# Gather of four experts at a time in float32, scatter from one float32 y buffer, and a new layout of SBUF, in a two-layer decoder trunk with 64 routed experts

## The reference

```
y = concat(mixer heads, memory heads) @ w_out[i]
x = layer_norm(ALPHA * x + y)
aff = sigmoid(x @ w_router[i]); the best 8 of 64 experts within the best 4 of 8 groups
gates = aff of the chosen / their sum * 2.5
routed = sum over chosen experts of gate * ((silu(x @ w_gate[e]) * (x @ w_up[e])) @ w_down[e])
shared = (silu(x @ ws_gate) * (x @ ws_up)) @ ws_down
x = layer_norm(ALPHA * x + routed + shared)
```

## Time and profile before

| | |
|---|---|
| three runs | 1184.29, 1184.86, 1186.17 us |
| median | 1184.86 us |
| profiled execution, its span | 1183.3 us |
| PE busy | 1149.2 us (97%) |
| weight loads busy (PEld) | 688.0 us (58%) |
| VectorE, ScalarE, GpSimd busy | 347.2, 300.0, 56.4 us |
| read from HBM | 446.96 MB, 379 GB/s over the span |
| chain that ended last | PE 85%, DMA 9%, DVE 3%, ACT 1% |

### The profile page before, as it was taken

The page is one execution under the profiler, slowest core; times in us unless marked ns, Lnnn a source line. Parts: engine busy times, 40 slices in busy tenths (PEclk is TensorE's granted clock), DMA queues, the critical chain, the costliest instruction groups (busy, mean ns, idle before and its releaser), DMA issues.

```text
span 1183.3 us, 22174 instructions
## 1 busy us (share of the span) xinstructions
PE 1149.2 (97%) x8846; PEld 688.0 (58%) x8846; DVE 347.2 (29%) x912; ACT 300.0 (25%) x713; POOL 56.4 (5%) x100
## 2 busy tenths in 40 slices
PE   9999999999999999999999999999999899999995
PEld 6865755555555555554787647555555555555552
DVE  0445522222122212121523557221222222121224
ACT  1454222212122212121214533122221212221222
POOL 1431100000001000000011001000000010000000
PEclk9999999999999999999999999999999999999998
DMA  9945999999999999999990558999999999999995
GB/s 375 418 161 185 349 418 426 428 428 428 429 428 421 429 426 427 426 426 418 406 364 2 230 233 343 408 426 426 429 429 428 428 423 427 426 426 428 428 423 204
DMA packets 42732, 449.12 MB, mean 380 GB/s; under 512 B 4512, under 2 KB 4896, under 8 KB 14240
## 3 DMA queue, kind: packets, MB, share of 16 engines
q1 hardware_dynamic: 41648, 443.30, 89.8%
q10 hardware_dynamic: 1008, 4.73, 1.0%
HBM read 446.96 MB, written 1.05 MB: 379 GB/s over the span
## 4 chain that ended last, share of the span: by engine, by line
PE 85%; DMA 9%; DVE 3%; ACT 1%; issue 1%; DVEq 0%; SPq 0%; ACTq 0%
PE bank L1301 18%; PE bank L1328 17%; PE bank L1364 17%; PE bank L848 7%; PE bank L867 6%; PE bank L1372 5%; PE bank L906 4%; DMA store<-in_w_gate 4%; DMA store<-in_w_down 3%; DMA store<-in_w_in_b 2%; PE bank L1337 2%; PE bank L1196 1%; PE bank L1066 1%; PE bank L1077 1%; ACT work L1498 1%
## 5 line engine op out<-in xcount | busy, mean ns | idle before, releaser
L1301 PE MATMUL bank<-store,work 128*64 128x256 f32 x1984 | 227.8, 382 | 5.3 <-DMA store<-in_w_gate 5.3
L1328 PE MATMUL bank<-store,work 128*64 128x256 f32 x1952 | 225.3, 379 | 6.2 <-issue 6.2
L1364 PE MATMUL bank<-store,work 128*32 128x512 f32 x1888 | 218.4, 595 | 3.1 <-ACT work L1498 2.9
L1301 PEld LDWEIGHTS bank<-store,work 128*64 128x64 f32 x1984 | 137.0, 137 | 116.1 <-issue 41.1
L1328 PEld LDWEIGHTS bank<-store,work 128*64 128x64 f32 x1952 | 145.0, 137 | 75.7 <-issue 11.6
L2030 DVE SCALAR_TENSOR_TENSOR yhalf<-bank,gcol,yhalf 128x512 fp32r<-128x512 f32 x124 | 92.9, 751 | 219.1 <-ACT yhalf L1664 219.1
L2022 DVE TENSOR_TENSOR work<-work,bank 128x256 f32<-128x256 f32 x64 | 27.0, 422 | 346.9 <-PE bank L1328 346.9
L1664 ACT ACTIVATE yhalf<-bank,gcol 128x512 fp32r<-128x512 f32 x124 | 85.1, 688 | 172.1 <-PE bank L1364 172.1
L1364 PEld LDWEIGHTS bank<-store,work 128*32 128x32 f32 x1888 | 56.1, 109 | 122.4 <-issue 110.7
L1498 ACT ACTIVATE work<-bank 128x512 f32<-128x512 f32 (+4 forms) x177 | 78.0, 441 | 105.8 <-PE bank L848 47.3
L1498 ACT ACTIVATE back<-bank 128x128 fp32r<-128x128 bf16 x64 | 17.8, 278 | 282.0 <-PE bank L1269 282.0
(11 more groups left out here) (185 smaller groups left out, 822.7 us busy)
## 6 DMA issues: line engine op xcount, KB each, us to landing
store<-in_w_down SPq DMA_DIRECT2D x56, 2048.0 KB, 17.7
store<-in_w_gate SPq DMA_DIRECT2D x56, 2048.0 KB, 17.7
store<-in_w_up SPq DMA_DIRECT2D x52, 2048.0 KB, 19.2
store<-in_w_up SPq DMA_DIRECT2D x18, 1024.0 KB, 10.5
store<-in_w_gate SPq DMA_DIRECT2D x12, 1024.0 KB, 8.5
store<-in_w_in_b SPq DMA_DIRECT2D x3, 3072.0 KB, 22.4
store<-in_w_out SPq DMA_DIRECT2D x4, 2048.0 KB, 14.2
store<-in_w_down SPq DMA_DIRECT2D x6, 1024.0 KB, 11.7
```

The source lines that it names most:

```text
L1301: last = pe.matmul(gate_bank[slots_of(e), 0:HID], xg[:, k, slots_of(2 * j + e)], w[e][:, k, :], start=(k == 0), stop=(k == KT - 1))
L1328: last = pe.matmul(up_bank[slots_of(e), 0:HID], xg[:, k, slots_of(2 * j + e)], w[e][:, k, :], start=(k == 0), stop=(k == KT - 1))
L1364: last = pe.matmul(yb[half][rows_of(t, e), :], hT[b][:, f, slots_of(e, t)], w[e][:, f, half * 512:half * 512 + 512], start=(f == 0), stop= ...
```

## The change

x stays one float32 tensor in SBUF for the whole kernel; its columns stand in chunk order (the host permutes x, w_out, w_down, w_shared_down and the norm's rows, and the last norm writes the result back in column order into `x_out`). The float32r halves, `x_high`, `x_low` and GpSimd's sum are gone. The gather takes four experts at a time ("quad"), twice per octet, in units 1 and 3, each as float32 products with 128 moving columns; its four banks hold two chunks each. Slots lie by tile first in `xg`, so gate and up take one product per tile and expert: 32 stationary columns, 32 products each.

```diff
-                def gather(O, backs, bank_of_chunk=gather_bank):
+                def gather(Q, backs, banks_of=gather_bank):
...
-                        for t in range(TT):
...
-                            last = product(banks[bank_of_chunk[k]][:, t * 256:(t + 1) * 256],
-                                           [(xhalf[:, part, t, k * P:(k + 1) * P], hot8[:, t, :]) for part in range(2)])
+                        for i in range(2):
+                            k = 2 * c + i
+                            for t in range(TT):
+                                first = i * 256 + t * P
+                                last = pe.matmul(banks[banks_of[c]][:, first:first + P], x[:, t, k * P:(k + 1) * P], hot4[:, t, :],
+                                                 start=True, stop=True)
                         last.then_inc(s_("gathered"), 1)
...
                         for e in range(2):
-                            last = pe.matmul(gate_bank[slots_of(e), 0:HID], xg[:, k, slots_of(2 * j + e)], w[e][:, k, :],
-                                             start=(k == 0), stop=(k == KT - 1))
+                            for t in range(TT):
+                                last = pe.matmul(gate_bank[slots_of(e, t), 0:HID], xg[:, k, gathered_slots(j, e, t)], w[e][:, k, :],
+                                                 start=(k == 0), stop=(k == KT - 1))
```

```diff
-                    for n in range(2):
-                        for t in range(TT):
-                            pe.matmul(sums[2 * t + half][:], back[b][rows_of(t), :],
-                                      yhalf[rows_of(t), n, half * 512:half * 512 + 512], start=False, stop=False)
+                    for t in range(TT):
+                        pe.matmul(sums[2 * t + half][:], back[b][rows_of(t), :], y[rows_of(t), half * 512:half * 512 + 512],
+                                  start=False, stop=False)
...
                 def scatter(U, b):
-                    pe.wait_ge(s_("y_parted"), 2 * U + 2)
-                    for half in range(2):
-                        scatter_half(half, b)
+                    pe.wait_ge(s_("y_act"), U + 1)
+                    scatter_half(0, b)
+                    pe.wait_ge(s_("y_dve"), U + 1)
+                    scatter_half(1, b)
...
-                    ahead = j == OCT_PAIRS - 1
+                    ahead = b == 1
```

```diff
+            def keep_late(l, part, e):
+                w = (w_gate, w_up)[part][l, LATE_PAIR, :, e, :]
+                sp.dma_start(late_view(part, e), by_k(w)).then_inc(sem("late"), 16)
...
+                filled(sp, G[l, "y2"])
+                keep(l, 2, 0)
+                keep_late(l, 0, 0)
                 used(sp, (l, "out1"))
...
+                keep_late(l, 0, 1)
                 sp.wait_ge(sem("normed"), 2 * TT * l + TT)
-                load_up_apart(l)
                 keep(l, 1, 0)
...
+                sp.wait_ge(sem(f"shared_gu_{l}"), TT)
+                load_up_apart(l)
                 keep(l, 1, 1)
```

The last norm's second half writes with a stride:

```diff
+                    last = dve.scalar_tensor_tensor(out=by_column(x_out[:, t, :])[:, :, ms], in0=by_chunk(x[:, t, :])[:, :, ms],
+                                                    scalar=rstd[:, t, :], in1=by_chunk(lnrow[:, 1, :])[:, :, ms],
                                                     op0=ALU.mult, op1=ALU.add)
```

More of the change, by code:

```diff
@@ L183, in build_trunk @@
[L183 to L189 removed]
+        kT = work[:, 0:1536].rearrange("p (t n) -> p t n", n=SEQ)
@@ L618, in _ @@
                 if l == 0:
[L619 to L632 removed]
+                    first_layer()
+                else:
+                    second_layer(extra)
@@ L905, in out_part @@
                         done = y_done[n] = y_done[n] + 1
-                        last = pe.matmul(bank_at(g)[:], mixT[:, c, t * P:(t + 1) * P],
-                                         item_view((l, f"out{half}"), 512)[:, c, :], start=start, stop=(done == KT))
+                        last = pe.matmul(bank_at(g)[:], mixT[:, c, t * P:(t + 1) * P], wo[:, c, :], start=start, stop=(done == KT))
                         if done == KT:
@@ L1413, in unit @@
                     rs = 2 * O + j // 2
+                    late = shared == 0
+                    gathers = rs + 1
                     if shared in (1, 2):
                         pe.wait_ge(sem(f"shared_hT_{l}"), r * TT + (shared + 1))
-                    gate(U, O, j, rs, kept, place)
+                    gate(U, O, j, rs, kept, place, late)
                     if place == 0:
```

513 lines of the change are left out of this document (262 added, 251 removed).

## The result

The changed kernel takes 1258.49 us (median of 4 runs, 1258.12 to 1259.01), against 1184.76 us for the kernel before in the same rounds (1184.29 to 1186.17). The ratio is 1.0621, with a 95% interval of 1.0605 to 1.0636: 73.7 us more. The forecast was 1254 us, in a range of 1244 to 1280.

The account below looks back on a forecast made before the run. TensorE was taken as the bound nearly everywhere, DMA 10% slower in the loop but with a stock. Terms 47.0 + 42.8 - 9.3 - 11.5 - 0.9 + 1.5 = +69.6 us on 1184.9 gave 1254 us, range 1244 to 1280.

Parts of the forecast that it names:

- DMA's deficit: Expert loop: weight loads fall behind TensorE by 5.4 us per octet, 58.7 against 53.33 us; 0.4 after the change.
- Gather: Expert loops: 15 gathers per layer at 3.6 us replace 7 at 4.32; both layers +47.0 us.
- Scatter: Expert loops: float32 scatter takes 1.8 us instead of 1.12, in 62 units; +42.8 us.
- with the change of shape behind it 1.8: Scatter: four float32 pairs take 1.72 us, and 1.8 us with the change of shape that follows.
- Gate, up and down: Expert units: the change from 32 to 64 stationary columns goes, -0.15 us in each of 62 units; -9.3 us.
- Waits for weights: Expert loops: TensorE's waits before gate and up vanish as its octet grows to 58.3 us; -11.5 us.
- 3 MB less per layer are read inside the loop: Waits term: three kept matrices take 3 MB per layer out of the loop's loads, 7.3 us at 429 GB/s.
- The rest: Outside the main terms: -0.9 us of TensorE waits, +1.5 us for the last norm's strided write, no wait from load order.
- (a): Rival, gate and up: TensorE cannot take instructions fast enough, gate 3.90 us instead of 3.46; +56 us, 1310 us; chance 0.10.
- (b): Rival, expert loops: DMA is the true bound, 6.3 million bytes less save 14.7 us, 1170 us; chance 0.03.
- (c): Rival, gather and scatter: float32 forms cost about what float32r cost, 1170 us; chance 0.02.
- (d): Rival, gather or new load order: late copies or shared weights cause waits, +21 us, 1275 us; chance 0.10.

Follow-up runs that it names:

- the kernels with and without the shape: Kernel before with float32 scatter and wide float32 gather: with gate and up products of 32 columns 1251.49 us, without 1261.05 us.
- the two float32 experiments: Kernel before with one edit each: float32 scatter alone, 1219.70 us; float32 gather alone, still eight experts wide, 1211.06 us.
- the run without the kept matrices: Changed kernel without the three matrices it keeps for pair 24, which load as any other pair's: 1258.74 us.
- the experiment with 32 columns: Kernel before with gate and up products of 32 columns instead of 64, nothing else: 1192.72 us, ratio 1.0061.

## Why the prediction came out right, point by point

The verdict is the forecast's: TensorE sets the end, DMA's deficit vanishes, 1258.5 against 1254. By its terms:

- **Gather, +47.0.** 3.6 us was taken for a narrow one, 3.58 measured. Per layer 15 x 3.58 - 7 x 4.32 = +23.5 us. The first gather of layer 0, with gate's wait for the last copy, takes 133.82 - 129.14 = 4.68 us against 4.87; 4.6 was forecast. Together +46.6. The price was read from six records of another stage, and held.

```profile
129.14 3.81 PE L1311 MATMUL bank<-router_work,x 128*128 128x128 f32 x32
133.82 3.66 PE L1361 MATMUL bank<-ring,router_work 128*32 128x256 f32 x64 [0.87 <-DVE router_work L1792]
```

- **Scatter, +42.8.** This term was mis-sized. Measured are 1.92 us a scatter, not 1.8, so 0.80 and not 0.68 us a unit: 49.6 us, and 50.2 with the last half. Four pairs at 0.43 us were right in themselves. The step that failed is "with the change of shape behind it 1.8": 0.20 us lie beyond the four pairs, not 0.08, 7.4 us in 62 units. The prediction put the change of shape ahead of the scatter at nothing. The starts of the second and of the last pair, and of what follows, show both:

```profile
236.57 0.59 PE L1433 MATMUL bank<-router_work 64*128 64x512 f32 x2
...
237.43 0.60 PE L1433 MATMUL bank<-router_work 64*128 64x512 f32 x2
```

The pair in the middle takes 0.43 us (236.57 to 237.00, and to 237.43), the first one 236.57 - 236.04 = 0.53 and the last one 237.96 - 237.43 = 0.53: 0.10 us at each end. The float32r scatter of the kernel before has the same 0.10 at each end (medians of its 62: first pair 0.34 us, last 0.33, the others 0.23). So the 1.12 us held it already: four pairs at 0.23 are 0.93. The term's own upper bound (1.95 us, 51 us) held it.
- **Gate, up and down, -9.3.** Unit rows give -0.16, the kernels with and without the shape -0.154: 9.6 us. Right, and at the place named: down to gate lost 0.11 us, gate to up 0.06. The kernel before with this shape alone has the same steps, 3.46, 3.45 and 3.57 us. That it is the change between 32 and 64 columns that costs is argued from the place.
- **Waits for weights, -11.5.** All gone, as forecast, but there was more to give back: 13.9 us within the loops. The step took the list's lengths as the time lost; the two float32 experiments show that they are too short. (The first wait came at 305.65 us, 0.34 listed, and not at 315.) "3 MB less per layer are read inside the loop" is so, but the forecast did not need it: the stock holds without them, as the run without the kept matrices shows. An octet of 58.64 against 58.7 us was forecast as 58.3.
- **The rest, +0.6.** Together the stretches outside the loops changed by -0.3 us: before the first loop -0.3, between the loops -1.1, tail +1.1. The tail's strided operations are there as priced (2.06 us, and 2.10 for the two halves):

```profile
1248.62 2.06 DVE L1816 SCALAR_TENSOR_TENSOR home<-x,rstd,lnrow 128x1024 f32<-128x1024 f32 x1
...
1252.02 2.10 DVE L1816 SCALAR_TENSOR_TENSOR home<-x,rstd,lnrow 128x512 f32<-128x512 f32 x2
```

With the measured sizes: 46.6 + 50.2 - 9.6 - 13.9 - 0.3 = 73.0 us, against 73.2 of span. That the forecast's 69.6 lies only 3.4 below this is partly luck: the scatter was 7.4 too low, and waits (2.4), the rest (0.9), gather (0.4) and gate (0.3) erred the other way.

**Rivals.** (a), that TensorE is bound by issue in gate and up, is refuted over the whole loop: 64 records from 245.47 to 248.92, 3.45 us, 54 ns each. The Trainium skill, in TensorE: Matmul & The Clock Gate, section "Wait — 56ns, not 53.3ns?", has about 62 ns per matmul as a bound with hardware decode off. No such bound shows here, with one record every 54 ns; but no run shows whether that decoding was off, or whether a float32 product counts there as one matmul or as its two records, so the rule itself is not tested. (b), DMA as the true bound, is refuted for this change, and its 14.7 us for 6.3 million bytes less rested on bytes that are read all the same (449.12 MB before, 449.56 after). Yet the experiment with 32 columns shows the part of it that was true: in the kernel before, that gain of TensorE was lost to DMA. (c), float32 at the price of float32r, is refuted by both single edits. (d), new waits, did not come, but for the 1.7 us after the two first gathers that the gather's term held: TensorE is idle 22.0 us of the span (1256.5 - 1234.5), where it was 34.1.

**What would beat both kernels** was not found, and no version was run for it. The experiments point to more weights loaded ahead with both multiplications left in float32r, since the kernel before loses 13.9 us to DMA; that is a guess. The change makes its room for kept matrices by dropping the low part of x and of y, which is what costs 97 us of TensorE; the float32r versions need those places.

## What to carry to other kernels

Where two resources are both near their limit, price an edit against the slack between them: a slower TensorE first fills its waits (13.9 us here, once, however many edits share it), and a faster one gained nothing here. Read what a wait costs from starts, against the same step without a wait: the listed waits were a sixth too short. Buffers that only move a load earlier save no bytes, and are worth something only once the stock ahead runs out; ask whether the edit that makes their room has not already removed the shortage. And an operation that is taken out may have been the cover for another engine's step, as the scatter was for VectorE's 0.42 us.

## What the runs showed of the hardware

- A float32 product costs by its columns, and twice over for its two records: 0.43 us a record with 512 columns, 0.215 with 256, 0.11 with 128 (3.58 / 32), against 0.13 us for a float32r record of 256 columns. Two float32r parts are cheaper than one float32 product at both widths that were run: 1.12 against 1.92 us in the scatter (512 columns), 4.32 against 6.91 in the wide gather (256).
- Four products of 32 stationary columns each, in a round, take no longer than two of 64 (3.45 against 3.50 us for 16 rounds). The gain of 0.154 us a unit lies mostly where down and gate meet, 3.46 against 3.57 us.
- The scatter of 64-row products has 0.20 us beyond its four pairs, 0.10 at its entry and 0.10 behind it, in float32 as in float32r.
- A wait for weights can be listed under "issue", and is listed from the modelled end of the record before it: 2.4 of 13.9 us lost lay under such ends.
